# Expert weights in another row order: eight (or four) consecutive rows to a partition

## Chip, cores and metric

One core of a Trainium2 chip runs the whole program in one launch. The metric is the device time in microseconds. TensorE (PE) does the matmuls, VectorE (DVE) and ScalarE (ACT) the elementwise work, GpSimd (POOL) the gathers, and SyncE (SP) issues most loads.

## What is computed

Two transformer blocks on 1024 tokens of 1024 features, all in f32. Around the change it is the first block's modulation and its mixture of experts:

```python
mod = silu(c) @ w_ada + b_ada
shift1, scale1, gate1, shift2, scale2, gate2 = split(mod, 6)
...
h2 = rmsnorm(x, norm2_w) * (1 + scale2) + shift2
...
g = argmax(softmax(h2 @ w_group + b_group))          # 4 groups of 8 experts
e = top_2(softmax(logits of the experts of group g))
xs = h2[tokens sorted by expert]
hid = silu(xs @ w1[e]) * (xs @ w3[e])                # w1, w3: (32, 1024, 512)
ys = (hid @ w2[e]) * gate                            # w2: (32, 512, 1024)
x = x + gate2 * sum_of_the_two(ys)
```

The second block has neighbourhood attention, gated linear attention and a dense MLP. The change does not touch it.

## The kernel before

Everything is tiled to 128 partitions: T = 1024 tokens are NT = 8 tiles, D = 1024 features are NK = 8 tiles, an expert's inner width DE = 512 is four tiles. The program is a sequence of stages. Each ends with a barrier of all engines (meet, line 144); inside a stage the engines run beside each other and wait on semaphores.

**Modulation** (lines 197 to 280). SP loads w_ada in 24 pieces of 1 MB (wa, line 223), and DVE adds each, times silu(c), into acc, 128 partitions by 6144 columns (line 248). TensorE then sums over the partitions: for each of 32 groups of 128 columns a matmul with acc as the stationary operand and a column of ones as the moving one, which gives one column of bank 0 (line 265); after that four matmuls of 512 columns for the two gates (line 270). DVE copies the columns to mod (line 252) and the gates (line 256), and affine_vector makes scale and shift columns of them (lines 278 and 279), with the norm's weights from cols. Column f of such a table holds features 128 f to 128 f + 127, one to a partition.

**Expert pass** (lines 1484 to 1696). The tokens are sorted by expert into blocks of 128 rows, at most 48; how many are in use is known only at run time, and the engines skip the others. For each block:

- SP loads the expert's w1, w3 and w2 (lines 1520, 1521, 1525), 2 MB each, into one of two sets of buffers, and may do so as soon as the block two before has used them. rows (line 1519) reads row 128 k + p of a matrix into partition p, place k: for w1 and w3 a partition gets eight pieces of 2 KB, for w2 four pieces of 4 KB.
- POOL gathers the block's 128 rows of normed x from DRAM (line 1544).
- TensorE turns the rows, eight transposes (experts_turn, line 1553, through the helper transposes, line 346). In a transpose the data is the stationary operand and the identity the moving one. ACT and DVE apply scale and shift while they copy the result to xsT (lines 1624, 1626).
- TensorE multiplies by w1 and w3 in two parts of 256 inner columns each (line 1587, xsT stationary, the weights moving), ACT and DVE make hid, TensorE turns hid (line 1592) and multiplies by w2 (line 1606); the next block's rows are turned between the two halves of hid.

The order on TensorE is the order of the code: up product, half of hid, next block's rows, other half, down product. Names of the trace: e_w is w1, w3 or w2, e_rows the gathered rows, e_xsT the turned ones, e_hid and e_hidT the inner values, mod_acc is acc. An f32 matmul leaves two records of PE and two of its weight load (PEld), a transpose one of each. The first tile named behind the arrow is the moving operand.

The lines that give the two orders before:

```python
rows = lambda w: io[w][ds(e, 1)].squeeze(0).rearrange("(k p) f -> p k f", p=P)
...
t = pe.matmul(experts_up_bank(k, part, j), b.xsT[n][:, f, :], w[:, f, part * HALF:(part + 1) * HALF], start=f == 0, stop=f == NK - 1)
```

Of the kernel before, what the change touches and what calls it, by code (L numbers as in the profile page):

```python
# [11 lines left out]
ALU = mybir.AluOpType  # L12
ACT = mybir.ActivationFunctionType
AX = mybir.AxisListType
ds = bass.ds
# [217 lines left out]
def modulation_vector(k, s, b, mod, gates):  # L233

    v = k.nc.vector
    loaded = (s.wa_0, s.wa_1, s.wa_2, s.wa_3, s.wa_4, s.wa_5)
    v.memset(b.acc[:, :], 0.0).then_inc(*s.acc_zero.up().inc)
    v.wait_ge(*s.acc_zero(1))
    v.wait_ge(*s.ada_bias(1))
    v.wait_ge(*s.c_silu(1))  # L240
    for i in range(NK):
        for j in range(3):
            n = 3 * (i % 2) + j
            v.wait_ge(*loaded[n](i // 2 + 1))
            if i:
                v.wait_ge(*s.ada_step(3 * (i - 1) + j + 1))
            part = b.acc[:, j * 2 * D:(j + 1) * 2 * D]
            v.scalar_tensor_tensor(part, b.wa[n][:, :], b.cT[:, i:i + 1], part, ALU.mult, ALU.add).then_inc(*s.ada_step.up().inc)
    v.wait_ge(*s.columns_made(1))
    for j in (0, 3):  # L250
        part = slice(j * NK, (j + 2) * NK)
        v.tensor_copy(mod[:, part], k.bank[0][:, part]).then_inc(*k.V.up().inc)
    for n in range(2):
        for h in range(2):
            v.wait_ge(*s.gate_made(2 * n + h + 1))
            v.tensor_copy(gates[n][:, h * BANK:(h + 1) * BANK], k.bank[1 + 2 * n + h][:, :]).then_inc(*k.V.up().inc)


def modulation_tensor(k, s, b):

    pe = k.nc.tensor
    pe.wait_ge(*s.ada_step(3 * NK))
    columns = [j for j in range(6 * NK) if j // NK not in (2, 5)]
    for j in columns:
        t = pe.matmul(k.bank[0][:, j:j + 1], b.acc[:, j * P:(j + 1) * P], k.c("ones")[:, 0:1], start=True, stop=True)
    t.then_inc(*s.columns_made.up().inc)
    for n, at in ((0, 2), (1, 5)):
        for h in range(2):
            cols = slice(at * D + h * BANK, at * D + (h + 1) * BANK)
            t = pe.matmul(k.bank[1 + 2 * n + h][:, :], k.c("ones"), b.acc[:, cols], start=True, stop=True)  # L270
            t.then_inc(*s.gate_made.up().inc)


def affine_vector(k, affine, mod, cols):

    v = k.nc.vector
    for n, j in ((0, 0), (1, 3)):
        v.scalar_tensor_tensor(affine[:, 2 * n, :], mod[:, (j + 1) * NK:(j + 2) * NK], 1.0, cols[:, n, :], ALU.add, ALU.mult).then_inc(*k.V.up().inc)
        v.tensor_copy(affine[:, 2 * n + 1, :], mod[:, j * NK:(j + 1) * NK]).then_inc(*k.V.up().inc)
    k.meet()  # L280

# [61 lines left out]
def transposes(k, bank, src, n=4):  # L343

    for h in range(n):
        t = k.nc.tensor.transpose(bank[:, h * P:(h + 1) * P], src[:, h * P:(h + 1) * P], k.c("ident"))  # L346
    return t
# [1158 lines left out]
def experts_sync(k, s, b, experts):  # L1506

    sy, io = k.nc.sync, k.io
    used = used_blocks(sy, experts)
    up, gate, down = (s.up_loaded_0, s.up_loaded_1), (s.gate_loaded_0, s.gate_loaded_1), (s.down_loaded_0, s.down_loaded_1)  # L1510
    for at in range(BLOCKS):
        n = at % 2
        there = used > at
        e = sy.value_load(experts[0:1, at:at + 1], min_val=0, max_val=NE - 1)
        if at >= 2:
            sy.wait_ge(*s.up_made(4 * (at - 1)))
            sy.wait_ge(*up[n](at // 2))
            sy.wait_ge(*gate[n](at // 2))
        rows = lambda w: io[w][ds(e, 1)].squeeze(0).rearrange("(k p) f -> p k f", p=P)
        sy.dma_start(b.w1[n][:, :, :], rows("w1"), cond=there, bounds_check="skip_entire_dma").then_inc(*up[n].up().inc)  # L1520
        sy.dma_start(b.w3[n][:, :, :], rows("w3"), cond=there, bounds_check="skip_entire_dma").then_inc(*gate[n].up().inc)
        if at >= 2:
            sy.wait_ge(*s.down_made(at - 1))
            sy.wait_ge(*down[n](at // 2))
        sy.dma_start(b.w2[n][:, :, :], rows("w2"), cond=there, bounds_check="skip_entire_dma").then_inc(*down[n].up().inc)
    for n in range(2):
        sy.wait_ge(*up[n].now())
        sy.wait_ge(*gate[n].now())
        sy.wait_ge(*down[n].now())
# [20 lines left out]
def experts_turn(k, s, b, n, half):  # L1550

    out = (s.half_0_turned, s.half_1_turned)[half]
    transposes(k, k.bank[half], b.rows[n][:, half * BANK:(half + 1) * BANK]).then_inc(*out.up().inc)


HALF = DE // 2
# [2 lines left out]
def experts_up_bank(k, part, j):  # L1559

    return k.bank[((2, 3), (7, 4))[part][j]][:, 0:HALF]


def experts_tensor(k, s, b, experts):
# [7 lines left out]
    for at in range(BLOCKS):  # L1572
        n = at % 2
        with pe.If(used > at):
            pe.wait_ge(*up[n](at // 2 + 1))
            pe.wait_ge(*s.half_0_out(4 * (at + 1)))
            pe.wait_ge(*s.half_1_out(4 * (at + 1)))
            for part in range(2):
                for j, w in enumerate((b.w1[n], b.w3[n])):
                    if part == 0 and j:  # L1580
                        pe.wait_ge(*gate[n](at // 2 + 1))
                    if at:
                        pe.wait_ge(*(s.hid_ready if j else s.silu_ready)(2 * (at - 1) + part + 1))
                    if at and part == 0 and j == 0:
                        pe.wait_ge(*s.hidT_out(2 * at))
                    for f in range(NK):
                        t = pe.matmul(experts_up_bank(k, part, j), b.xsT[n][:, f, :], w[:, f, part * HALF:(part + 1) * HALF], start=f == 0, stop=f == NK - 1)  # L1587
                    t.then_inc(*s.up_made.up().inc)
            for part in range(2):
                pe.wait_ge(*s.hid_ready(2 * at + part + 1))  # L1590
                for f in (2 * part, 2 * part + 1):
                    t = pe.transpose(k.bank[2 + part][:, f % 2 * P:(f % 2 + 1) * P], b.hid[:, f * P:(f + 1) * P], k.c("ident"))
                t.then_inc(*s.hid_turned.up().inc)
                if part == 0:
                    pe.wait_ge(*got[1 - n]((at + 1) // 2 + 1))
                    experts_turn(k, s, b, 1 - n, 0)
                    experts_turn(k, s, b, 1 - n, 1)
            pe.wait_ge(*down[n](at // 2 + 1))
            for part in range(2):
                pe.wait_ge(*s.hidT_out(2 * at + part + 1))  # L1600
                if at and part == 0:
                    pe.wait_ge(*s.y_out_a(at))
                    pe.wait_ge(*s.y_out_v(at))
                for h in range(2):
                    for f in (2 * part, 2 * part + 1):
                        t = pe.matmul(k.bank[5 + h][:, :], b.hidT[:, f * P:(f + 1) * P], b.w2[n][:, f, h * BANK:(h + 1) * BANK],  # L1606
                                      start=f == 0, stop=f == DE // P - 1)
            t.then_inc(*s.down_made.up().inc)
        with pe.Else():
            pe.drain()  # L1610
            pe.sem_inc(s.up_made.sem, 4)
            pe.sem_inc(s.half_0_turned.sem, 1)
            pe.sem_inc(s.hid_turned.sem, 2)
            pe.sem_inc(s.half_1_turned.sem, 1)
            pe.sem_inc(s.down_made.sem, 1)
# [804 lines left out]
def build(nc, io, out):  # L2420

    with ExitStack() as ctx:
# [9 lines left out]
        xn_rows, y_rows = dram("xn_rows", T, D), dram("y_rows", BLOCKS * P, D)  # L2432
        x_rows = [dram(f"x_rows{n}", T, D) for n in range(3)]
        rpb_rows = dram("rpb_rows", NAH, 2 * KH - 1, W, 2 * W - 1)
        cols = sb("cols", P, 4, NK)
        load_constants(k, consts, cols)

        hT = sb("hT", P, NK, T)
        routed = ctx.enter_context(ExitStack())
        of = lambda name, *shape, dt=F32: routed.enter_context(k.area(name, shape, dt))  # L2440
        mod, affine, gate1, gate2 = of("mod", P, 6 * NK), of("affine", P, 4, NK), of("gate1", P, D), of("gate2", P, D)
        gates, where, tokens, experts = of("gates", P, NT, 2), of("where", P, NT, 2, dt=U32), of("tokens", P, BLOCKS + 1, dt=U32), of("experts", P, BLOCKS + 1, dt=I32)
        with Areas(k) as area:
            x = area("x_first", P, NT, D)
# [15 lines left out]
            store_rows(k, x, x_rows[0])  # L2460
            norm_transpose(k, x, hT, affine[:, 2, :], affine[:, 3, :], xn_dram=xn_rows)
        route(k, hT, gates, where, tokens, experts)
        experts_pass(k, affine[:, 2, :], affine[:, 3, :], tokens, experts, xn_rows, y_rows)
        with Areas(k) as area:
            norm_w, x = area("final_w", P, D), area("x_routed", P, NT, D)
            load_vector(k, norm_w, io["final_norm_w"])
# [23 lines left out]
def arrays_of(inputs):  # L2490
# [7 lines left out]
    io["b_ada"] = a["b_ada"].reshape(1, -1)  # L2498
    io["cT"] = by_feature(a["c"].reshape(-1))
    io["positions"] = a["positions"].reshape(NT, P).T  # L2500
    io["norm_columns"] = np.stack([by_feature(a[n].reshape(-1)) for n in ("norm1_w", "norm2_w", "ln_mix_g_2", "ln_ff_g_2")], 1)
    io["conv"] = a["conv_w"][0].reshape(4, 12, P).transpose(2, 1, 0)
    for n, src in (("a_log", "a_log"), ("dt_bias", "dt_bias"), ("dn_norm_w", "dn_norm_w"), ("b_group", "b_group"),
                   ("b_expert", "b_expert"), ("final_norm_w", "final_norm_w"), ("ln_final_g_2", "ln_final_g_2"),
# [21 lines left out]
```

## Time and profile before

| | us |
|---|---|
| median of 3 runs | 4374.59 |
| lowest, highest | 4372.19, 4376.29 |
| the profiled execution | 4376.07 |
| its span, first to last instruction | 4374.3 |
| modulation, from its last addition on DVE to the last affine column | 85.2 to 105.9 |
| expert pass, first gather's index to the next stage's first load | 1469.9 to 2299.3 |

The profile is of one execution. The span is the time between its first and last instruction; the profiled execution's own time is 1.8 us longer. "Busy" is the time in which an engine executes something; matmuls are pipelined, so the pace of a stream of them is read from the starts of groups in the timeline and not from the mean of one. The granted clock is a share of TensorE's full 2.4 GHz.

### The profile page before, as it was taken

What the parts mean: (1) busy time and instruction counts of PE and PEld (TensorE: products, weight loads), DVE (VectorE), ACT (ScalarE), POOL (GpSimd) and SP (SyncE); (2) the same over time, 40 slices, a digit from 0 to 9 for tenths busy, and PEclk for the clock granted to TensorE, in tenths of its full rate; (3) what the DMA queues carried; (4) which work ended last, traced back from release to release, by engine and by line L of the source; (5) the groups of instructions that cost most, each with busy time, mean ns of one, the idle gap of its engine ahead of it and who ended that gap; (6) DMA issues with size and microseconds to landing.
All of it is one profiled execution on the core that took longest, in us unless ns stands there. A gap on an engine that the chain in (4) does not pass through costs nothing. (4 is left out here: it accounts for less than half of the span.)

```text
span 4374.3 us, 31822 instructions
## 1 busy us (share of the span) xinstructions
PE 3570.6 (82%) x12530; PEld 2143.0 (49%) x12530; DVE 1055.8 (24%) x2157; ACT 697.0 (16%) x1576; POOL 186.1 (4%) x215
## 2 busy tenths in 40 slices
PE   1697789677777699999961877889656899999999
PEld 1344454566634577777741335543443444444444
DVE  6203213444412311111105015600562200000101
ACT  0201101222201122222212015500210100000000
POOL 0002000111000000000011000000000000000000
PEclk9798889777877699999985888899667999999999
DMA  6113411000022598899954210010002111122222
GB/s 282 39 39 49 160 25 34 1 1 1 1 77 79 209 343 334 334 334 334 334 201 158 57 38 1 1 58 5 1 1 77 59 38 39 39 77 86 87 82 77
DMA packets 223732, 457.98 MB, mean 105 GB/s; under 512 B 27120, under 2 KB 80912, under 8 KB 220368
## 3 DMA queue, kind: packets, MB, share of 16 engines
q1 hardware_dynamic: 207409, 396.48, 26.8%
q0 software_dynamic: 9360, 34.08, 2.1%
q10 hardware_dynamic: 6800, 25.17, 1.4%
q8 instruction: 111, 1.82, 0.2%
q14 instruction: 52, 0.43, 0.0%
HBM read 479.43 MB, written 66.82 MB: 125 GB/s over the span
## 5 line engine op out<-in xcount | busy, mean ns | idle before, releaser
L1587 PE MATMUL bank<-e_w,e_xsT 128*128 128x256 f32 x2240 | 492.3, 381 | 6.7 <-DMA e_w<-in_w 6.7
L1587 PEld LDWEIGHTS bank<-e_w,e_xsT 128*128 128x128 f32 x2240 | 427.4, 191 | 80.5 <-issue 16.3
L2316 PE MATMUL bank<-w_ff,uT 128*128 128x512 f32 x1024 | 441.8, 594 | 2.6 <-DVE hT L2368 2.6
L2299 PE MATMUL bank<-hT,w_ff 128*128 128x512 f32 x1024 | 439.7, 592 | 1.3 <-DVEq L149 1.3
L2316 PEld LDWEIGHTS bank<-w_ff,uT 128*128 128x128 f32 x1024 | 195.0, 191 | 249.1 <-issue 244.1
L2299 PEld LDWEIGHTS bank<-hT,w_ff 128*128 128x128 f32 x1024 | 194.5, 190 | 245.9 <-issue 244.4
L464 PE MATMUL bank<-w_out,mixT 128*128 128x512 f32 x512 | 225.0, 603 | 44.0 <-DMA w_out<-in_w_out 44.0
L1606 PE MATMUL bank<-e_w,e_hidT 128*128 128x512 f32 x560 | 246.1, 592 | 0.0
L464 PE MATMUL bank<-w_in,hT 128*128 128x512 f32 x512 | 221.6, 596 | 24.1 <-DMA w_in<-in_w_in 24.1
L346 PE MATMUL bank<-consts,norm_xn 128*128 128x128 f32 x256 | 56.8, 414 | 193.9 <-DVE norm_xn L401 193.9
L464 PEld LDWEIGHTS bank<-w_out,mixT 128*128 128x128 f32 x512 | 99.0, 194 | 169.2 <-issue 169.2
L464 PE MATMUL bank<-w_gla,hT 128*128 128x512 f32 x384 | 166.6, 597 | 11.3 <-DMA w_gla<-in_w_in 11.3
L734 PE MATMUL bank<-hT,w_qkv 128*128 128x512 f32 x384 | 168.6, 598 | 8.6 <-DMA w_qkv<-in_w_in 8.6
L464 PEld LDWEIGHTS bank<-w_in,hT 128*128 128x128 f32 x512 | 97.8, 191 | 147.4 <-issue 147.4
L1606 PEld LDWEIGHTS bank<-e_w,e_hidT 128*128 128x128 f32 x560 | 103.7, 190 | 117.2 <-issue 117.2
L346 PEld LDWEIGHTS bank<-consts,norm_xn 128*128 128x128 f32 x256 | 51.4, 223 | 201.3 <-issue 144.9
L1683 DVE TENSOR_TENSOR e_hid<-e_act,bank 128x256 f32<-128x256 f32 x70 | 29.5, 421 | 455.8 <-PE bank L1587 455.8
L2359 DVE TENSOR_TENSOR uT<-uT,bank 128x512 f32<-128x512 f32 x64 | 41.1, 684 | 400.7 <-ACT uT L2334 400.7
L734 PE MATMUL bank<-hT,w_nqk 128*128 128x512 f32 x256 | 113.0, 605 | 16.9 <-DMA w_nqk<-in_w_in 16.9
L464 PEld LDWEIGHTS bank<-w_gla,hT 128*128 128x128 f32 x384 | 73.5, 192 | 103.8 <-issue 103.8
L734 PEld LDWEIGHTS bank<-hT,w_qkv 128*128 128x128 f32 x384 | 72.9, 192 | 96.4 <-issue 96.4
L2368 DVE TENSOR_TENSOR hT<-hT,bank 128x512 f32<-128x512 f32 x16 | 10.7, 684 | 410.7 <-PE bank L2316 410.6
(448 smaller groups left out, 3967.0 us busy)
## 6 DMA issues: line engine op xcount, KB each, us to landing
e_w<-in_w SPq DMA_DIRECT2D x144, 2048.0 KB
w_ff<-in_w_ff SPq DMA_DIRECT2D x96, 512.0 KB
wa<-in_w_ada SPq DMA_DIRECT2D x24, 1024.0 KB, 12.6
y_rows<-e_y ACTq DMA_DIRECT2D x48, 512.0 KB
y_rows<-r_zero SPq DMA_DIRECT2D x1, 16384.0 KB
w_in<-in_w_in SPq DMA_DIRECT2D x4, 2048.0 KB
w_out<-in_w_out SPq DMA_DIRECT2D x4, 2048.0 KB, 10.5
x_rows<-x_mixed SPq DMA_DIRECT2D x2, 4096.0 KB, 12.8
```

The lines of the kernel that those rows point to most:

```text
L346: t = k.nc.tensor.transpose(bank[:, h * P:(h + 1) * P], src[:, h * P:(h + 1) * P], k.c("ident"))
L464: t = pe.matmul(k.bank[m][:, :], xT[:, f, m * P:(m + 1) * P], wbuf[at % 2][:, f, :], start=f == 0, stop=f == NK - 1)
L734: t = pe.matmul(k.bank[2 * (n % 2) + h][:, :], wbuf[n % 2][:, f, :], xT[:, f, h * BANK:(h + 1) * BANK], start=f == 0, stop=f == NK - 1)
L1587: t = pe.matmul(experts_up_bank(k, part, j), b.xsT[n][:, f, :], w[:, f, part * HALF:(part + 1) * HALF], start=f == 0, stop=f == NK - 1)
L1606: t = pe.matmul(k.bank[5 + h][:, :], b.hidT[:, f * P:(f + 1) * P], b.w2[n][:, f, h * BANK:(h + 1) * BANK], start=f == 0, stop=f == DE // P ...
L1683: v.tensor_tensor(b.hid[:, cols], b.act[:, cols], experts_up_bank(k, part, 1), ALU.mult).then_inc(*s.hid_ready.up().inc)
L2299: t = pe.matmul(k.bank[2 * (j % 2) + h][:, :], w[:, f, :], hT[:, f, h * BANK:(h + 1) * BANK], start=f == 0, stop=f == NK - 1)
L2316: t = pe.matmul(k.bank[2 * n + h][:, :], uT[:, f, m * P:(m + 1) * P], b.ring[j % SLOTS][:, h * BANK:(h + 1) * BANK], start=f == 0, stop=f ...
L2359: v.tensor_tensor(dst, dst, k.bank[2 * (j % 2) + h][:, :], ALU.mult).then_inc(*s.u_ready.up().inc)
L2368: v.tensor_tensor(dst, dst, k.bank[2 * (m % 4) + h][:, :], ALU.add).then_inc(*s.x_added.up().inc)
```

## The change

The weights of an expert are loaded in another row order, and all that depends on it follows:

- rows reads row 8 p + k (w1, w3) or 4 p + k (w2) into partition p, place k. A partition's eight or four rows are one contiguous piece of 16 KB.
- Feature tile f of the block's rows must then hold features f, 8 + f, 16 + f, ...: experts_turn reads every eighth column of the gathered rows.
- Inner tile q must hold inner columns q, 4 + q, ...: the up product reads every fourth column of w1 and w3.
- The affine columns of the expert pass are needed in the new feature order. 16 more column matmuls in the modulation, which read every eighth column of acc, a third copy to mod, and two more operations in affine_vector make them; cols gets a fifth column set. The tables for route and the norm stay.

```diff
-    for j in (0, 3):
+    for j in (0, 3, 6):
         part = slice(j * NK, (j + 2) * NK)
         v.tensor_copy(mod[:, part], k.bank[0][:, part]).then_inc(*k.V.up().inc)
...
     for j in columns:
-        t = pe.matmul(k.bank[0][:, j:j + 1], b.acc[:, j * P:(j + 1) * P], k.c("ones")[:, 0:1], start=True, stop=True)
+        pe.matmul(k.bank[0][:, j:j + 1], b.acc[:, j * P:(j + 1) * P], k.c("ones")[:, 0:1], start=True, stop=True)
+    for j in range(2 * NK):
+        at = (3 + j // NK) * D + j % NK
+        t = pe.matmul(k.bank[0][:, 6 * NK + j:6 * NK + j + 1], b.acc[:, at:at + D - j % NK:NK], k.c("ones")[:, 0:1], start=True, stop=True)
     t.then_inc(*s.columns_made.up().inc)
...
-    for n, j in ((0, 0), (1, 3)):
-        v.scalar_tensor_tensor(affine[:, 2 * n, :], mod[:, (j + 1) * NK:(j + 2) * NK], 1.0, cols[:, n, :], ALU.add, ALU.mult).then_inc(*k.V.up().inc)
+    for n, j, w in ((0, 0, 0), (1, 3, 1), (2, 6, 4)):
+        v.scalar_tensor_tensor(affine[:, 2 * n, :], mod[:, (j + 1) * NK:(j + 2) * NK], 1.0, cols[:, w, :], ALU.add, ALU.mult).then_inc(*k.V.up().inc)
         v.tensor_copy(affine[:, 2 * n + 1, :], mod[:, j * NK:(j + 1) * NK]).then_inc(*k.V.up().inc)
...
-        rows = lambda w: io[w][ds(e, 1)].squeeze(0).rearrange("(k p) f -> p k f", p=P)
+        rows = lambda w: io[w][ds(e, 1)].squeeze(0).rearrange("(p k) f -> p k f", p=P)
...
-    transposes(k, k.bank[half], b.rows[n][:, half * BANK:(half + 1) * BANK]).then_inc(*out.up().inc)
+    for q in range(4):
+        f = half * 4 + q
+        t = k.nc.tensor.transpose(k.bank[half][:, q * P:(q + 1) * P], b.rows[n][:, f:f + D - NK + 1:NK], k.c("ident"))
+    t.then_inc(*out.up().inc)
...
-                        t = pe.matmul(experts_up_bank(k, part, j), b.xsT[n][:, f, :], w[:, f, part * HALF:(part + 1) * HALF], start=f == 0, stop=f == NK - 1)
+                        columns = w[:, f, :].rearrange("p (c q) -> p q c", q=4)[:, 2 * part:2 * part + 2, :]
+                        t = pe.matmul(experts_up_bank(k, part, j), b.xsT[n][:, f, :], columns, start=f == 0, stop=f == NK - 1)
...
-        experts_pass(k, affine[:, 2, :], affine[:, 3, :], tokens, experts, xn_rows, y_rows)
+        experts_pass(k, affine[:, 4, :], affine[:, 5, :], tokens, experts, xn_rows, y_rows)
```

On TensorE at the start of the program, where the columns (mod_acc stationary) and the gates (mod_acc moving) are made, the order before is

```order
L265 MATMUL bank<-consts,mod_acc 128x1 x32
L270 MATMUL bank<-mod_acc,consts 128x512 x4
L346 MATMUL bank<-consts,norm_xn_1 128x128 x64
L464 MATMUL bank<-w_in_1,hT 128x512 x256
L346 MATMUL bank<-consts,r_qk_1 128x128 x16
```

and with the change

```order
L265 MATMUL bank<-consts,mod_acc 128x1 x32
L268 MATMUL bank<-consts,mod_acc 128x1 x16
L273 MATMUL bank<-mod_acc,consts 128x512 x4
L349 MATMUL bank<-consts,norm_xn_1 128x128 x64
L467 MATMUL bank<-w_in_1,hT 128x512 x256
L349 MATMUL bank<-consts,r_qk_1 128x128 x16
```

The 16 new matmuls stand between the old columns and the gates; what follows is in the old order, at line numbers three higher and more.

On TensorE in the expert pass, from the branch that begins block 0, the order before is

```order
L346 MATMUL bank<-consts,e_rows_1 128x128 x8
L1574 COMPARE_AND_BRANCH
L1587 MATMUL bank<-e_w_1,e_xsT_1 128x256 x32
L1592 MATMUL bank<-consts,e_hid 128x128 x2
L346 MATMUL bank<-consts,e_rows_1 128x128 x8
L1592 MATMUL bank<-consts,e_hid 128x128 x2
L1606 MATMUL bank<-e_w_1,e_hidT 128x512 x8
L1574 UNCONDITIONAL_BRANCH
L1609 UNCONDITIONAL_BRANCH
L1574 COMPARE_AND_BRANCH
```

and with the change

```order
L1558 MATMUL bank<-consts,e_rows_1 128x128 x8
L1580 COMPARE_AND_BRANCH
L1594 MATMUL bank<-e_w_1,e_xsT_1 128x256 x32
L1599 MATMUL bank<-consts,e_hid 128x128 x2
L1558 MATMUL bank<-consts,e_rows_1 128x128 x8
L1599 MATMUL bank<-consts,e_hid 128x128 x2
L1613 MATMUL bank<-e_w_1,e_hidT 128x512 x8
L1580 UNCONDITIONAL_BRANCH
L1616 UNCONDITIONAL_BRANCH
L1580 COMPARE_AND_BRANCH
```

Number, kinds and order are the same; the turned rows now come from the loop in experts_turn and not from the helper transposes.

## Rows read from the trace of the kernel before

**Rows 1.** The page, parts 1 and 2: busy time, and the clock in 40 slices.
```profile
span 4374.3 us, 31822 instructions
...
PE 3570.6 (82%) x12530; PEld 2143.0 (49%) x12530; DVE 1055.8 (24%) x2157; ACT 697.0 (16%) x1576; POOL 186.1 (4%) x215
...
PEclk9798889777877699999985888899667999999999
```

**Rows 2.** Windows, two stretches: stretch, length, busy by engine, granted clock, DMA share, GB/s.
```profile
1522.00:1544.00 22.00, 22.00 (x93) 16.47 (x93) 2.90 (x7) 4.81 (x10) 1.15 (x2) 1.00 1.04 400
1600.00:1800.00 200.00, 200.00 (x840) 149.99 (x839) 26.08 (x63) 43.65 (x91) 10.29 (x18) 1.00 0.90 335
```

**Rows 3.** Timeline of PE, a block: start, us, engine, line, operation, tiles, shapes, count.
```profile
1508.86 13.98 PE L1587 MATMUL bank<-e_w,e_xsT 128*128 128x256 f32 x64
1522.67 0.38 PE L1592 MATMUL bank<-consts,e_hid 128*128 128x128 f32 x2
1522.89 1.04 PE L346 MATMUL bank<-consts,e_rows 128*128 128x128 f32 x8
...
1523.98 7.03 PE L1606 MATMUL bank<-e_w,e_hidT 128*128 128x512 f32 x16
1530.85 13.98 PE L1587 MATMUL bank<-e_w,e_xsT 128*128 128x256 f32 x64
```

**Rows 4.** The page, part 5: the costliest group, its count and mean.
```profile
L1587 PE MATMUL bank<-e_w,e_xsT 128*128 128x256 f32 x2240 | 492.3, 381 | 6.7 <-DMA e_w<-in_w 6.7
```

**Rows 5.** Waits of PE from 1470 to 2257 us: total, times, longest.
```profile
PE bank L1587 <- DMA e_w<-in_w: 6.7, 2, 6.0
PE bank L346 <- DMA e_rows<-xn_rows,e_idx: 5.6, 1, 5.6
```

**Rows 6.** Timeline of all engines, start of the expert pass.
```profile
1470.32 1.15 POOL L1544 DMA_INDIRECT e_rows<-xn_rows,e_idx  x1 [0.29 <-POOL e_idx L1542]
...
1471.54 0.42 SPq L1520 DMA_DIRECT2D e_w<-in_w  x1
...
1475.10 1.97 PE L346 MATMUL bank<-consts,e_rows 128*128 128x128 f32 x8 [5.64 <-DMA e_rows<-xn_rows,e_idx]
...
1477.11 1.37 DVE L1624 TENSOR_SCALAR e_xsT<-bank,affine 128x128 f32<-128x128 f32 x4 [7.40 <-PE bank L346]
...
1483.07 6.49 PE L1587 MATMUL bank<-e_w,e_xsT 128*128 128x256 f32 x16 [5.99 <-DMA e_w<-in_w]
...
1490.22 10.63 PE L1587 MATMUL bank<-e_w,e_xsT 128*128 128x256 f32 x48 [0.66 <-DMA e_w<-in_w]
```

**Rows 7.** Timeline of all engines, end of the modulation.
```profile
85.35 13.73 PEld L265 LDWEIGHTS bank<-consts,mod_acc 128*128 128x128 f32 x64 [85.35 <-issue]
...
99.03 5.59 PE L270 MATMUL bank<-mod_acc,consts 128*128 128x512 f32 x8
...
105.49 0.17 DVE L278 SCALAR_TENSOR_TENSOR affine<-mod,cols 128x8 f32<-128x8 f32 x1
...
105.73 0.16 DVE L279 COPY affine<-mod 128x8 f32<-128x8 f32 x1
```

**Rows 8.** Packets and bytes, 30 to 60 us, 1490 to 1500 us, 1471 to 1484 us.
```profile
DMA packets 1738, 12.66 MB, mean 422 GB/s; under 512 B 193, under 2 KB 193, under 8 KB 193
...
DMA packets 1627, 3.94 MB, mean 394 GB/s; under 512 B 31, under 2 KB 31, under 8 KB 1627
...
DMA packets 1730, 4.20 MB, mean 323 GB/s; under 512 B 50, under 2 KB 50, under 8 KB 1730
...
q1 hardware_dynamic: 1327, 2.68, 57.9%
q0 software_dynamic: 403, 1.51, 32.6%
```

**Rows 9.** Timeline of POOL, a gather in mid-pass, and its tile's time to landing.
```profile
1502.46 0.96 POOL L1544 DMA_INDIRECT e_rows<-xn_rows,e_idx  x1 [0.27 <-POOL e_idx L1542]
...
DMA to landing us min/median/max: 4.1/7.8/8.9
```

More of the change, by code:

```diff
@@ L2434, in build @@
         rpb_rows = dram("rpb_rows", NAH, 2 * KH - 1, W, 2 * W - 1)
-        cols = sb("cols", P, 4, NK)
+        cols = sb("cols", P, 5, NK)
         load_constants(k, consts, cols)
@@ L2440, in build @@
         of = lambda name, *shape, dt=F32: routed.enter_context(k.area(name, shape, dt))
-        mod, affine, gate1, gate2 = of("mod", P, 6 * NK), of("affine", P, 4, NK), of("gate1", P, D), of("gate2", P, D)
+        mod, affine, gate1, gate2 = of("mod", P, 8 * NK), of("affine", P, 6, NK), of("gate1", P, D), of("gate2", P, D)
         gates, where, tokens, experts = of("gates", P, NT, 2), of("where", P, NT, 2, dt=U32), of("tokens", P, BLOCKS + 1, dt=U32), of("experts", P, BLOCKS + 1, dt=I32)
@@ L2500, in arrays_of @@
     io["positions"] = a["positions"].reshape(NT, P).T
-    io["norm_columns"] = np.stack([by_feature(a[n].reshape(-1)) for n in ("norm1_w", "norm2_w", "ln_mix_g_2", "ln_ff_g_2")], 1)
+    io["norm_columns"] = np.stack([by_feature(a[n].reshape(-1)) for n in ("norm1_w", "norm2_w", "ln_mix_g_2", "ln_ff_g_2")] + [vec("norm2_w").reshape(P, NK)], 1)
     io["conv"] = a["conv_w"][0].reshape(4, 12, P).transpose(2, 1, 0)
```

## Prediction

> **What bounds the kernel now.** I read the page first: one core, a span of 4374.3 us, TensorE busy for 3570.6 us of it, and a clock that is granted in full over the middle of the span [rows 1]. The change touches two places, so I then asked for each by itself: the expert pass (1470 to 2299 us) and the modulation at the start (85 to 106 us).
>
> In the expert pass the windows show TensorE busy 200.00 us of 200.00, at a granted clock of 1.00 (2.4 GHz), while the DMA engines are at 0.90 and move 335 GB/s [rows 2]. The timeline of PE gives the pulse: one block's up product starts at 1508.86 us and the next at 1530.85, so a block takes 21.99 us, and the rows between join without a gap [rows 3]. There are 35 blocks in use: 2240 records of L1587 [rows 4] at 64 a block (32 matmuls, two records each for f32). The table of waits says what TensorE waited for in the whole pass: 6.7 us, in two waits, for expert weights, and 5.6 us for the first gathered rows [rows 5]. So **the whole of what faster weight loads can give in this pass is 6.7 us**, 0.15% of the span; all other loads of weights already land under matmuls. What can cost is any change in what TensorE itself does, 35 times over.
>
> In the modulation nothing overlaps: DVE waits for the column matmuls, then for the gate matmuls, then makes the affine columns, and a barrier holds everybody. What TensorE needs longer there is longer for the kernel [rows 7].
>
> **The change, part by part.**
>
> *Loads in one piece of 16 KB a partition (w1, w3, w2).* In mid-pass: nothing. The load rate is not what a block waits for. After the start the engines catch up at 400 GB/s with pieces of 2 and 4 KB [rows 2], more than the 335 GB/s that a block's pulse asks for. At the start of the pass there is something to win. w1's first load is issued at 1471.54 us and TensorE starts on it at 1483.07; w3 costs 0.66 us more at 1490.22 [rows 6]. The nearest rows for the rate are these: pieces of 2 and 4 KB at 394 GB/s (1490 to 1500 us), pieces of 8 KB in the w_ada loads at 422 GB/s (30 to 60 us), and 4.20 MB moved between 1471 and 1484 us, of which 1.51 MB for gathers [rows 8]. The lower bound of the gain is 0. The upper is 4.6 + 0.7 = 5.3 us: the turned rows are ready at 1477.11 + 1.37 = 1478.48 us [rows 6], so w1 cannot be used before that, 4.6 us earlier than now. I take −1.5 us: 2.68 MB of queue 1 at 422 in place of 394 GB/s saves 0.45 us, the second wait of 0.66 goes, and 0.4 because larger pieces take a larger share from the gathers beside them. The other side of this last point is that the gathers land later. In mid-pass they have the time: one is issued at 1502.46 us, lands after a median of 7.8 us, and is first needed at 1522.89 [rows 3, 9]. The first gather landed at 1475.10 and could slip some 3 us before w1 is no longer last.
>
> *Turned rows (L346 in the pass becomes a loop in experts_turn).* As many transposes, with a stationary operand whose 128 elements lie 32 bytes apart in place of side by side. Now 12 transposes take 1523.98 − 1522.67 = 1.31 us, 0.109 us each [rows 3]. Lower bound 0, upper bound: the weight load takes twice as long and shows in full, 8 × 0.109 × 35 = 31 us. I take 0, for the reason under the next edit.
>
> *Inner columns (L1587).* As many matmuls, but the moving operand reads every fourth element, 16 bytes apart. One record of 256 columns now takes 13.98 / 64 = 0.218 us, one of 512 columns (L1606) 6.87 / 16 = 0.429 us [rows 3]: 0.82 ns for a column of f32, two cycles of the 2.4 GHz clock. No matmul in this trace has a step in its operands, so both ends stay open. Lower bound 0; upper bound, each element takes twice as long: 2240 × 0.218 = 489 us. I take 0. TensorE takes an element only every second cycle, and it does so wherever the clock is granted; the slack for another address is there. That is an inference from the pace, not a row, and it is the weakest step. The Trainium skill speaks against it: "Advanced Engine Details and Errata", section "SBUF Cachelines", says that lines have 16 bytes and that at least two hits on a line are needed to hide the access latency. Here each f32 element would be the only hit on its line; by that rule the upper bound of 489 us, not zero, is the one to take, which makes the sum about +495 us, and no row here shows it.
>
> *Modulation.* It gets 16 more column matmuls of one column, 32 records. The 64 records there now take 13.73 us on the weight-load side, 0.2145 us each [rows 7]; 32 more are +6.9 us on the path. Bounds: at the pace of the fast transposes, 0.109, only +3.5; with the step of 32 bytes in the weight load costing double, +13.7. I take 6.9, since these rows are the same instruction in the same place. On DVE a third copy to mod hides while DVE waits for the gate matmuls; the two more affine operations add 0.16 us (four of them start between 105.49 and 105.73). Sum **+7.0 us**. The cols load is 4 KB larger: nothing.
>
> *Experts' affine columns, hid, w2 and y.* The same shapes on the same engines, with other numbers inside: 0.
>
> *The end of the pass* (the unused blocks) skips the loads of weights, so they cannot shorten it.
>
> **Sum:** +7.0 − 1.5 = +5.5 us. The profiled execution took 4376.07 us (span 4374.3) and would become 4381.6; the median of the three runs, 4374.59, lies 1.5 us below that execution, so the forecast for the median is 4380. I call 0.2% (8.75 us) what a measurement of this kernel can tell from no change. So the forecast is: no change that can be told, on the slow side. Own range of this case: 4374 to 4386.
>
> **Rivals.**
>
> 1. *Slower: the stepped moving operand.* Place: L1587 (L1594 in the changed kernel). Price: 0.218 us for each of 2240 records if reading at a step of 16 bytes halves the pace, 489 us, and with the weight loads of the turned rows (31) and of the modulation (6.9) it is 527: 4380 + 527 = 4907. It decides from about 2% of loss per matmul on (2% of 489 is 9.8 us). For it: no row shows a stepped operand at the present pace. Against it: two cycles per element. Chance 0.12. (The rule of the Trainium skill quoted above, "SBUF Cachelines", would make this case the forecast.)
>
> 2. *Slower, the weight load alone.* Only the stationary operand at 32 bytes is slow, while the moving one is not: 31 + 6.9 = 38 us more, 4418. The transposes have no long matmul to hide a weight load under, which the up product has. Chance 0.08.
>
> 3. *Slower, in between.* Either a partial loss on the moving operand (10% is 49 us: 4429), or the loads of 16 KB run slower than those of 2 KB because 128 pieces that lie 16 KB apart suit the memory less. That decides below 335 GB/s; at 300 a block would need 24.6 us, 35 × 2.6 = 90 us: 4470. Nothing in the trace speaks for the latter, pieces of 8 KB being the fastest [rows 8]. Chance 0.06.
>
> 4. *Faster.* The start of the pass gives its full 5.3 us and the added column matmuls cost 3.5 + 0.2: −1.6 us, 4373. Still no change that can be told. To be faster by over 8.75 us more must go than TensorE ever waits for in the pass, so this holds only what I do not see, chance 0.05 in all. That the larger pieces do nothing for the loads at all is inside the forecast: 4381.5.
>
> **How the numbers follow.** The forecast has 0.69, the rivals 0.12, 0.08, 0.06 and 0.05. The forecast's case lies within 0.2% but for some 0.02 at its slow end. Faster 0.04, same 0.68, slower 0.28. The range takes the forecast's case with its bounds and rival 2, and leaves out rivals 1 and 3 (0.18): 4370 to 4420. It is 4380 because that is the likeliest case, not a mean.
>
> **What would show it.** Right: a block's pulse still 21.99 us and 64 records of the up product in 13.98; 12 transposes in 1.31 us; 96 weight-load records of about 0.2145 us in the modulation, with its gate matmuls starting near 105.9 us in place of 99.03; TensorE's first up product 1 to 2 us sooner after w1's issue, and the second wait gone; the packets of queue 1 fewer by tens of thousands. Wrong: a pulse over 22 us without a wait (rival 1 or 2, told apart by which rows are longer), or one with waits for DMA inside the pass (rival 3); a modulation shorter than 12 us for its 96 records would make my largest term half as big.

## The result, and the profile after

| | before | changed |
|---|---|---|
| median us | 4375.44 (4 runs, 4372.19 to 4377.42) | 4906.86 (4 runs, 4904.24 to 4915.14) |
| ratio to before | | 1.1219, 95% interval 1.1199 to 1.1238 |
| profiled execution, its span | 4376.07, 4374.3 | 4904.24, 4902.4 |

The change makes the kernel 531 us slower. The page of the changed kernel, against [rows 1]: the span, busy times, the clock, and the packets of the queue that carries the weights.

```profile
span 4902.4 us, 31889 instructions
...
PE 4104.9 (84%) x12562; PEld 2189.4 (45%) x12562; DVE 1056.1 (22%) x2160; ACT 697.0 (14%) x1576; POOL 185.9 (4%) x215
...
PEclk9897798878869999999999859888976799999999
...
q1 hardware_dynamic: 131249, 396.48, 22.9%
```

TensorE is busy for 534 us more, with 32 records more. The clock is granted in full over more slices than before. The weights come in 131249 packets in place of 207409 on the page of before, so the loads did change as meant:

```profile
q1 hardware_dynamic: 207409, 396.48, 26.8%
```

The costliest group of the page is the up product, as in [rows 4]:

```profile
L1594 PE MATMUL bank<-e_w,e_xsT 128*128 128x256 f32 x2240 | 1021.4, 632 | 3.7 <-DMA e_w<-in_w 3.7
```

As many records, 2240, but a mean of 632 ns where it was 381. Ahead of them the engine waits 3.7 us in all. The timeline of PE shows the pulse of a block, to be laid beside [rows 3]:

```profile
1481.68 29.64 PE L1594 MATMUL bank<-e_w,e_xsT 128*128 128x256 f32 x64 [3.68 <-DMA e_w<-in_w]
...
1519.35 29.17 PE L1594 MATMUL bank<-e_w,e_xsT 128*128 128x256 f32 x64
1548.35 0.40 PE L1599 MATMUL bank<-consts,e_hid 128*128 128x128 f32 x2
1548.58 1.06 PE L1558 MATMUL bank<-consts,e_rows 128*128 128x128 f32 x8
1549.48 0.38 PE L1599 MATMUL bank<-consts,e_hid 128*128 128x128 f32 x2
1549.70 7.03 PE L1613 MATMUL bank<-e_w,e_hidT 128*128 128x512 f32 x16
1556.57 29.17 PE L1594 MATMUL bank<-e_w,e_xsT 128*128 128x256 f32 x64
```

From one up product to the next it is 1556.57 − 1519.35 = **37.22 us**, where it was 21.99. The up product itself goes from 13.81 us (1508.86 to 1522.67) to 29.00, so a record from 0.216 us to 0.453, 1.77 ns a column (paces are taken from start to start). The twelve transposes from 1548.35 to 1549.70 take 1.35 us, where they took 1.31. The windows and the waits of the pass (columns as in [rows 2, 5]) show that in mid-pass neither the clock nor a load is missing:

```profile
1481.00:1484.00 3.00, 2.32 (x5) 1.75 (x6) 0.00 (x0) 0.00 (x0) 0.00 (x0) 0.50 1.03 412
...
1600.00:1800.00 200.00, 200.00 (x492) 94.98 (x491) 14.92 (x36) 24.42 (x51) 5.72 (x10) 1.00 0.49 196
```

```profile
PE bank L1594 <- DMA e_w<-in_w: 3.7, 1, 3.7
```

In the middle TensorE is busy all the time at a clock of 1.00, while the DMA engines have fallen to half their time. The first load of the pass and the end of the modulation, as in [rows 6, 7]:

```profile
1472.51 0.36 SPq L1523 DMA_DIRECT2D e_w<-in_w  x1
```

```profile
85.18 13.73 PEld L265 LDWEIGHTS bank<-consts,mod_acc 128*128 128x128 f32 x64 [85.18 <-issue]
...
98.79 7.71 PEld L268 LDWEIGHTS bank<-consts,mod_acc 128*128 128x128 f32 x32
...
106.44 5.07 PE L273 MATMUL bank<-mod_acc,consts 128*128 128x512 f32 x8
...
113.03 0.16 DVE L282 COPY affine<-mod 128x8 f32<-128x8 f32 x1
```

The first load is issued at 1472.51 us and used at 1481.68, after 9.17 us in place of 11.53, and TensorE has no second wait of its own. The rows of 1490 to 1500 us, with the loads at full flow, as in [rows 8]:

```profile
DMA packets 309, 4.32 MB, mean 432 GB/s; under 512 B 43, under 2 KB 43, under 8 KB 46
```

That is 432 GB/s with pieces of 16 KB, against 394 with 2 and 4 KB and 422 with 8 KB.

**Where the 528.1 us of the spans lie.** The last affine column starts at 113.03 in place of 105.73: +7.3. From there to the first load of w1, in stages that the change doesn't touch, 1359.5 us against 1365.8: −6.3, the scatter of single executions. From that load to the first up product: −2.4. From the first up product to the end of the last down product 1303.1 us against 773.7 us: +529.4. After it 2117.6 against 2117.5: +0.1. Of the 529.4, 34 blocks give 34 × 15.22 = 517.5 and the first block 11.9, because before that block was slow too: it ran in part at a granted clock of 0.50.

### The profile page after: what moved, and what is told of

Same layout as the page of the kernel before. It is cut to its first block and busy times, and to the rows that moved or that the text cites. A ratio compares the mean times of both kernels' runs of the same rounds, so it can differ in the third digit from the quotient of the medians.

```text
span 4902.4 us, 31889 instructions
## 1 busy us (share of the span) xinstructions
PE 4104.9 (84%) x12562; PEld 2189.4 (45%) x12562; DVE 1056.1 (22%) x2160; ACT 697.0 (14%) x1576; POOL 185.9 (4%) x215
## 3 DMA queue, kind: packets, MB, share of 16 engines
q1 hardware_dynamic: 131249, 396.48, 22.9%
## 5 line engine op out<-in xcount | busy, mean ns | idle before, releaser
L1594 PE MATMUL bank<-e_w,e_xsT 128*128 128x256 f32 x2240 | 1021.4, 632 | 3.7 <-DMA e_w<-in_w 3.7
L1594 PEld LDWEIGHTS bank<-e_w,e_xsT 128*128 128x128 f32 x2240 | 467.4, 209 | 550.2 <-issue 544.3
L1653 ACT ACTIVATE e_act<-bank 128x256 f32<-128x256 f32 x70 | 26.8, 383 | 654.9 <-PE bank L1594 654.9
```

The lines of the kernel that those rows point to most:

```text
L1653: a.activation(b.act[:, part * HALF:(part + 1) * HALF], experts_up_bank(k, part, 0), ACT.Silu).then_inc(*s.silu_ready.up().inc)
```

## The experiments

The theory after the result (A): a moving operand with a step of 16 bytes is read at half the pace or less, and nothing else of the change matters. Rivals: the loads in large pieces disturb TensorE's reading (B); the pattern of two dimensions does it, not the step (C). The pulse of a block and the pace of its 64 records are the measure, since they don't depend on the stages ahead. All profile rows below are of PE's timeline, but for one of SP in experiment 1. Experiments 2 and 9 edit the kernel before, with its loads; the others edit the changed one and keep w1 and w3 in pieces of 16 KB. Experiments 2, 5, 6, 7 and 8 leave out what would make the columns match again, so their output is another one; the amount of work is the same. Where a kernel ran once, its rows carry the argument and not its time: the kernel before took 4368 to 4402 us in the 30 runs made beside experiments 1 to 6, 8 and 10.

**1. The step undone, the large pieces kept.**

```diff
-columns = w[:, f, :].rearrange("p (c q) -> p q c", q=4)[:, 2 * part:2 * part + 2, :]
+columns = w[:, f, part * HALF:(part + 1) * HALF]
...
+tiles = io["w2"][ds(e, 1)].squeeze(0).rearrange("(k p) f -> p k f", p=P)
...
-sy.dma_start(b.w2[n][:, :, :], rows("w2"), ...)
+sy.dma_start(b.w2[n][:, :, :], tiles, ...)
```

> The changed kernel with the inner columns undone: the up product reads 256 neighbouring columns of w1 and w3 as before, and w2 goes back to four pieces of 4 KB a partition to match. Loads of w1 and w3 stay in pieces of 16 KB, turned rows and modulation stay as changed. Theory A (all of the loss is the 16-byte step in the moving operand): one record of the up product back to 0.216 us, the pulse of a block at 22.03 us (the turned rows keep their 0.04), time 4375.4 + 7.4 for the modulation + 1.4 for the turned rows - 3 for the start of the pass = about 4381. Theory B (the loads of 16 KB pieces into the partitions that TensorE reads slow it down): the records stay near 0.45 us and the time near 4900.

Measured: 4376.7 us (10 runs) against 4372.11 (13 runs), ratio 1.0006, interval 0.9996 to 1.0015.

```profile
1472.86 0.36 SPq L1524 DMA_DIRECT2D e_w<-in_w  x1
...
1482.12 6.11 PE L1595 MATMUL bank<-e_w,e_xsT 128*128 128x256 f32 x16 [3.77 <-DMA e_w<-in_w]
1489.91 10.63 PE L1595 MATMUL bank<-e_w,e_xsT 128*128 128x256 f32 x48 [1.67 <-DMA e_w<-in_w]
...
1508.57 13.98 PE L1595 MATMUL bank<-e_w,e_xsT 128*128 128x256 f32 x64
1522.38 0.38 PE L1600 MATMUL bank<-consts,e_hid 128*128 128x128 f32 x2
...
1530.57 13.98 PE L1595 MATMUL bank<-e_w,e_xsT 128*128 128x256 f32 x64
```

The pulse is 22.00 us and the up product 13.81 us again. Theory B falls: with w1 and w3 in pieces of 16 KB TensorE keeps its old pace. One more thing shows here. w1 is used 9.3 us after its issue and not 11.5, but then TensorE waits 1.67 us for w3, so the start of the pass wins less than the first wait says: the second up product begins 1508.57 − 1472.86 = 35.71 us after the first load, where it was 1508.86 − 1471.54 = 37.32, 1.6 us less.

**2. The step alone, in the kernel before.**

```diff
-... b.xsT[n][:, f, :], w[:, f, part * HALF:(part + 1) * HALF], ...
+columns = w[:, f, :].rearrange("p (c q) -> p q c", q=4)[:, 2 * part:2 * part + 2, :]
+... b.xsT[n][:, f, :], columns, ...
```

> The kernel before with one edit: the up product reads every fourth column of w1 and w3. Loads, turned rows and modulation as before. It leaves the match with w2's rows out, so that the output is another one. Theory A: 0.453 us a record, 29.0 us for the up product of a block, a pulse of 37.2 us, time 4375 + 35 x 15.19 = about 4907. Theory B (the loads do it, not the step): 0.216 us a record and 4375.

Measured: one run, 4901.41 us.

```profile
1516.31 29.17 PE L1588 MATMUL bank<-e_w,e_xsT 128*128 128x256 f32 x64
1545.30 0.40 PE L1593 MATMUL bank<-consts,e_hid 128*128 128x128 f32 x2
...
1553.50 29.17 PE L1588 MATMUL bank<-e_w,e_xsT 128*128 128x256 f32 x64
```

28.99 us for the up product and a pulse of 37.19: this one edit makes the whole loss, with the loads of before. With experiment 1 this settles where it comes from.

**3. A step of 8 bytes.**

```diff
+pairs = io["w2"][ds(e, 1)].squeeze(0).rearrange("(t p k) f -> p t k f", t=2, k=2)
...
-columns = w[:, f, :].rearrange("p (c q) -> p q c", q=4)[:, 2 * part:2 * part + 2, :]
+columns = w[:, f, part * HALF:(part + 1) * HALF].rearrange("p (c q) -> p q c", q=2)
```

> The changed kernel with a step of two columns (8 bytes) in place of four (16 bytes); w2's rows are loaded to match, in two pieces of 8 KB. Theory A1 (the time goes by 16-byte lines, 1.77 ns for each new line, as measured at one element a line): two elements a line are 0.885 ns an element against 0.843 now, 0.227 us a record, a pulse of about 22.8 us, time about 4406. Theory A2 (any step at all, elements that are not neighbours, takes the slow way): 0.453 us a record, time about 4907. A3 (cost in proportion to the step): about 0.30 us a record, 4570.

Measured: one run, 4400.52 us.

```profile
1508.09 14.67 PE L1595 MATMUL bank<-e_w,e_xsT 128*128 128x256 f32 x64
1522.60 0.38 PE L1600 MATMUL bank<-consts,e_hid 128*128 128x128 f32 x2
...
1530.80 14.67 PE L1595 MATMUL bank<-e_w,e_xsT 128*128 128x256 f32 x64
```

14.51 us for 64 records, 0.2267 us each: A1's number. A step as such is not what costs (A2), nor does the cost grow in proportion (A3).

**4. Two dimensions without a step.**

```diff
+tiles = io["w2"][ds(e, 1)].squeeze(0).rearrange("(k p) f -> p k f", p=P)
...
-columns = w[:, f, :].rearrange("p (c q) -> p q c", q=4)[:, 2 * part:2 * part + 2, :]
+columns = w[:, f, :].rearrange("p (q h c) -> p h q c", q=2, h=2)[:, part, :, :]
...
-... b.w2[n][:, f, h * BANK:(h + 1) * BANK], ...
+... b.w2[n][:, f % 2 * 2 + f // 2, h * BANK:(h + 1) * BANK], ...
```

> The changed kernel with the moving operand in two dimensions as there (2 by 128), but without a step: two runs of 128 neighbouring columns, 256 apart; w2 in its old order, its tiles taken to match. Theory A: 0.216 us a record, time about 4381 as for the kernel without a step. Theory C (the pattern of two dimensions costs, not the step): 0.453 us a record, time about 4907.

Measured: one run, 4392.31 us.

```profile
1522.13 13.98 PE L1595 MATMUL bank<-e_w,e_xsT 128*128 128x256 f32 x64
1535.94 0.38 PE L1600 MATMUL bank<-consts,e_hid 128*128 128x128 f32 x2
```

The up product takes 13.81 us, so theory C falls. The time is 11 us above what was expected, and none of it is in the pass: its first up product starts at 1495.60 us and not at about 1482, behind stages that are the same in all these kernels. A single run's time can be that far off (4368 to 4402 us for the kernel before); the pulse of before is 21.99 us at each of its steady blocks.

**5. A step of 12 bytes.**

```diff
-columns = w[:, f, :].rearrange("p (c q) -> p q c", q=4)[:, 2 * part:2 * part + 2, :]
+whole = w[:, f, :]
+columns = bass.AP(whole.tensor, whole.offset + part, [list(whole.ap[0]), [P, 2], [3, P]])
```

> The changed kernel with a step of three columns (12 bytes) in the up product's moving operand: two runs of 128 elements, the second 128 columns on. It multiplies by columns that overlap and don't match w2, so that the output is another one. Theory A1 (1.77 ns for each new 16-byte line): four elements touch three lines, 0.75 x 1.77 = 1.33 ns an element, 0.34 us a record, 64 records in 21.8 us, a pulse of about 30.0 us, time about 4660. Theory A4 (full pace while at least one of two neighbours shares a line, else the slow way): between, a line with one element costs 1.77 and a line with two 1.69, the same 0.34. Theory A5 (every step above 8 bytes goes the slow way, element by element): 0.453 us a record, time about 4905.

Measured: one run, 4658.68 us.

```profile
1518.02 21.91 PE L1595 MATMUL bank<-e_w,e_xsT 128*128 128x256 f32 x64
1539.76 0.39 PE L1600 MATMUL bank<-consts,e_hid 128*128 128x128 f32 x2
...
1547.97 21.92 PE L1595 MATMUL bank<-e_w,e_xsT 128*128 128x256 f32 x64
```

21.74 us, 0.3397 us a record, where 0.75 lines an element at 1.77 ns gave 0.340 (A1). A5 falls. A4 is not "the same 0.34" when its own prices are multiplied out: two lines with one element and one with two are 2 × 1.77 + 1.69 = 5.23 ns for four elements, 0.335 us a record, and for a step of 8 bytes it has the full pace, 0.216, where experiment 3 measured 0.227. So A1 fits better, by 0.005 and 0.011 us a record.

**6. A step of 32 bytes.**

```diff
-columns = w[:, f, :].rearrange("p (c q) -> p q c", q=4)[:, 2 * part:2 * part + 2, :]
+columns = w[:, f, :].rearrange("p (c q) -> p q c", q=8)[:, 4 * part:4 * part + 4, :]
```

> The changed kernel with a step of eight columns (32 bytes) in the moving operand, four runs of 64; hid's columns no longer match w2's rows, so that the output is another one. Theory A1 (time by the line): each element is a new line as with 16 bytes, 0.453 us a record, a pulse of 37.2 us, time about 4905. Theory A3 (cost grows with the distance): clearly above, 0.6 us or more a record, time above 5200.

Measured: one run, 4922.13 us.

```profile
1518.49 29.69 PE L1594 MATMUL bank<-e_w,e_xsT 128*128 128x256 f32 x64
1547.99 0.40 PE L1599 MATMUL bank<-consts,e_hid 128*128 128x128 f32 x2
...
1556.21 29.68 PE L1594 MATMUL bank<-e_w,e_xsT 128*128 128x256 f32 x64
```

29.50 us, 0.461 us a record: twice the distance costs 1.7% more, not twice as much, and A1, which had 0.453, is off by that much. A3 falls for good. Since this operand is four runs of elements where the change has two, another kernel was made to tell the number of runs from the distance.

**7. The same with four runs.**

```diff
-columns = w[:, f, :].rearrange("p (c q) -> p q c", q=4)[:, 2 * part:2 * part + 2, :]
+columns = w[:, f, :].rearrange("p (h c q) -> p h q c", h=2, q=4)[:, :, 2 * part:2 * part + 2, :]
```

> The changed kernel with the same step of 16 bytes in the up product, but as four runs of 64 elements and not two of 128; hid's columns then don't match w2's rows, so that the output is another one. The step of 32 bytes in e6_step_8 also had four runs, and took 0.461 us a record and not 0.453. Theory H (each further run costs a few ns): 0.461 us, time about 4920. Theory I (the distance costs, not the run): 0.453 us, about 4905.

Measured: one run, 4916.16 us (the pass began 12 us later than in the changed kernel).

```profile
1531.96 29.18 PE L1594 MATMUL bank<-e_w,e_xsT 128*128 128x256 f32 x64
1560.96 0.40 PE L1599 MATMUL bank<-consts,e_hid 128*128 128x128 f32 x2
```

29.00 us: the number of runs costs nothing (H falls), so the 1.7% belong to the distance (I).

**8. The step on the stationary operand.**

```diff
-columns = w[:, f, :].rearrange("p (c q) -> p q c", q=4)[:, 2 * part:2 * part + 2, :]
+columns = w[:, f, part * HALF:(part + 1) * HALF]
+turned = b.xsT[n][:, :, :].rearrange("p k c -> p (k c)")[:, f:f + D - NK + 1:NK]
-... b.xsT[n][:, f, :], columns, ...
+... turned, columns, ...
```

> The kernel of e1_no_step with a step of 32 bytes in the up product's stationary operand in place of one in the moving one: it reads every eighth element of the turned rows, 128 of them. It mixes features, so that the output is another one. Theory D (the weight load reads stepped elements at nearly its own pace, as the turned rows' transposes at 0.112 us show, and hides under the matmul of 0.216 us): 0.216 us a record, a pulse of 22.0 us, time as e1_no_step, about 4377. Theory E (1.77 ns a line holds for the weight load as well): 128 elements take 0.227 us, longer than the matmul's 0.216, 64 records in 14.5 us, a pulse of 22.7 us, time about 4401.

Measured: one run, 4433.93 us.

```profile
1514.52 15.45 PE L1596 MATMUL bank<-e_w,e_xsT 128*128 128x256 f32 x64
1529.80 0.38 PE L1601 MATMUL bank<-consts,e_hid 128*128 128x128 f32 x2
...
1538.00 15.45 PE L1596 MATMUL bank<-e_w,e_xsT 128*128 128x256 f32 x64
```

15.28 us, 0.2388 us a record. Theory D falls and E holds in kind, though it had 0.227 us a record and 4401 us: 128 stepped elements of a weight load take 0.239 us (1.87 ns each, not 1.77), which no longer hides under the matmul's 0.216 us. It costs 1.47 us a block against 15.19, since the load has 128 stepped elements and not 256, and only what is longer than the matmul shows. The 32 added column matmuls of the modulation, whose stationary operand has the same step, give the same 0.238 us a record. D was drawn from the turned rows, and these are transposes.

**9. The step on the identity of the transposes.**

```diff
+k.nc.vector.tensor_copy(k.ident4[:, 0:4 * P - 3:4], k.c("ident")).then_inc(*k.V.up().inc)
...
-transposes(k, k.bank[half], b.rows[n][:, half * BANK:(half + 1) * BANK]).then_inc(*out.up().inc)
+    t = k.nc.tensor.transpose(k.bank[half][:, q * P:(q + 1) * P], b.rows[n][:, f * P:(f + 1) * P], k.ident4[:, 0:4 * P - 3:4])
```

> The kernel before, contiguous everywhere, but the turned rows' transposes take their moving operand, the identity, from a table with every element 16 bytes from the next (made by DVE at the start of the pass, with one more barrier). Theory F (a stepped read takes about 0.885 ns whoever makes it, and an f32 matmul reads each element of an operand twice, a transpose once): 128 x 0.885 = 0.113 us a transpose against 0.109, the eight of a block in about 0.91 us, a pulse of 22.03 us, time about 4378. Theory G (a stepped element costs the moving side 1.77 ns in any instruction): 0.227 us a transpose, eight in 1.8 us, a pulse of 22.9 us, time about 4408.

Measured: one run, 4408.4 us (the kernel before, once beside it, 4387.5).

```profile
1508.87 13.98 PE L1595 MATMUL bank<-e_w,e_xsT 128*128 128x256 f32 x64
...
1522.90 2.02 PE L1560 MATMUL bank<-e_ident,e_rows 128*128 128x128 f32 x8
1524.74 0.40 PE L1600 MATMUL bank<-consts,e_hid 128*128 128x128 f32 x2
...
1531.85 13.98 PE L1595 MATMUL bank<-e_w,e_xsT 128*128 128x256 f32 x64
```

The eight transposes take 1.84 us, 0.230 each, and the pulse is 22.98 us: theory G. That the time meets its 4408 us says little with one run. A moving operand pays some 1.8 ns for each stepped element in a transpose as in a matmul. The idea that an f32 matmul pays double because it reads everything twice and a transpose once (F) does not hold for the moving side. A stationary operand with 32 bytes pays 0.1125 us at most in a transpose (0.90 us for the eight in the changed kernel) and 0.239 in an f32 matmul; why these two differ stays open.

**10. Large pieces with every step on a transpose's stationary side.** w2 comes in pieces of 8 KB. The 16 added columns of the modulation are gone; the affine columns in the new order come through DRAM instead.

```diff
+pairs = io["w2"][ds(e, 1)].squeeze(0).rearrange("(t p k) f -> p t k f", t=2, k=2)
...
+columns = w[:, f, part * HALF:(part + 1) * HALF]
...
-pe.transpose(..., b.hid[:, f * P:(f + 1) * P], k.c("ident"))
+pe.transpose(..., b.hid[:, part * HALF + f % 2:(part + 1) * HALF - 1 + f % 2:2], k.c("ident"))
...
-for j in range(2 * NK):
-    at = (3 + j // NK) * D + j % NK
-    t = pe.matmul(k.bank[0][:, 6 * NK + j:6 * NK + j + 1], b.acc[:, at:at + D - j % NK:NK], k.c("ones")[:, 0:1], start=True, stop=True)
...
+k.nc.sync.dma_start(dram.rearrange("a (k p) -> p a k", p=P), affine[:, 2:4, :], ...)
+k.nc.sync.dma_start(affine[:, 4:6, :], dram.rearrange("a (p k) -> p a k", k=NK))
```

> A version that keeps large pieces and has no step in a moving operand: w1 and w3 in pieces of 16 KB, the up product contiguous, w2 in two pieces of 8 KB, hid turned with a step of two in the stationary operand, and the affine columns for the new order made without TensorE, by a small store and load through DRAM on SP under the first norm. Theory A: against before 0 for the modulation, -1.7 to -3 us for the start of the pass, +1.4 for the turned rows (35 x 0.04), about +0.5 for hid: 4371 to 4376 where before is 4374, no difference that can be told. Rival: TensorE never waited for loads but 6.7 us, yet the larger pieces also shorten other waits; then it is faster by more than 9 us.

Measured: 4374.75 us (12 runs) against 4380.08 (17 runs), ratio 0.9986, interval 0.9971 to 1.0002.

```profile
1501.41 13.98 PE L1602 MATMUL bank<-e_w,e_xsT 128*128 128x256 f32 x64
1515.23 0.39 PE L1607 MATMUL bank<-consts,e_hid 128*128 128x128 f32 x2
...
1523.46 13.98 PE L1602 MATMUL bank<-e_w,e_xsT 128*128 128x256 f32 x64
```

No difference that can be told from before. The interval, −12.7 to +0.9 us, does not shut out the rival's 9 us by itself; the trace does. The pulse is 22.05 us, 0.06 over before, 1.9 us in 34 blocks. Against that stand 1.3 us at the start of the pass: the second up product begins 36.04 us after the first load of w1 (issued at 1465.37 us) in place of 37.32. From that load to the end of the last down product it is 785.8 us where it was 785.2. So this order of the weights won nothing, in a pass where TensorE waits 6.7 us for them.

## Why the prediction was wrong

**The bound of the pass** was read rightly: TensorE sets the pulse, and faster loads can give at most the 6.7 us it waited. In experiments 1 and 10, with the loads changed and no step in a moving operand, the time is that of before.

**The step that failed** is the one under "Inner columns": "I take 0. TensorE takes an element only every second cycle [...] the slack for another address is there." It was called the weakest step, and it bore the forecast all the same. Measured: 0.453 us for a record in place of 0.216, 2240 times: 532 us, less 3 in the first block. The slack is not there. The pace of contiguous elements could not show it: at 0.84 ns each, four to a line of 16 bytes, they ask for a new line every 3.4 ns, and the step asks for one with every element. The runs fit a price of 1.77 ns for each new line, wherever that is more than the 0.84 ns of its elements: steps of 8, 12, 16 and 32 bytes give 0.227, 0.340, 0.453 and 0.461 us a record. The Trainium skill's rule ("Advanced Engine Details and Errata", section "SBUF Cachelines"), that at least two hits on a 16-byte line are needed, agrees in kind with these rows: with two elements a line the loss is 5%, with one it is 110%. The prediction quoted this rule as speaking against the change and gave it 0.12. (Its "0.82 ns for a column" is a slip: 0.429 us for 512 columns is 0.84. Its 0.218 us a record includes the modelled end of the group; from start to start it is 0.216. Neither moves the forecast.) With no row on either side, a stated rule that names this very pattern should have weighed more than an inference from the pace of contiguous reads.

**Rival 1** named the mechanism, the place and the sign of the profile (a longer pulse without a wait). Its 4907 us meet the 4906.86 measured partly by luck. It had +489 for the moving operand, where 35 × 15.19 = 532 less some 3 for the first block was measured; +31 for the turned rows, where at most 35 × 0.04 = 1.4 was; and +13.9 for the modulation, where +7.3 was. The untouched stages added −6.3 in the profiled execution. The first was too small, since the loss is to 2.1 times and not double, and the other two were too large.

**Turned rows**, taken at 0: right within 1.4 us. The twelve transposes take 0.04 us more a block; the pulse of the changed kernel is over that of experiment 2, whose rows are turned as before, by only 0.02 to 0.03 us (37.22 and 37.21 against 37.19).

**Modulation**, taken at +7.0: +7.3. The 32 added records take 7.6 us, 0.238 us each and not 0.2145; the gate matmuls behind them took 5.07 us and not 5.59, because TensorE came to its full pace after the third of their eight records and not after the fourth (0.85 us a record until then, 0.43 after it).

**Start of the pass**, taken at −1.5: −1.6 in experiment 1. w1 is used 2.3 us sooner after its issue and its 16 records take 0.4 less (6.11 us against 6.49), but 1.0 goes back into the wait for w3 (1.67 us against 0.66), which the prediction had as gone.

**The forecast's own case**, 4380, was +5.5 on before. Experiment 1 is that case but for w2's pieces: +4.6 on before in the medians, +2.6 by the ratio, with an interval of −1.7 to +6.6 us that holds both 0 and +5.5. So the times can't prove the small terms; the rows above bear them out. The step in the moving operand, taken at 0, put the result outside the range.

## What to carry to other kernels

Look at the innermost step of a moving operand before the loads: f32 elements 16 bytes apart more than double a matmul's time, 8 bytes apart cost 5%. If a layout needs a step somewhere, it belongs on the stationary side of a transpose, where 32 bytes cost 0.03 us for eight of them here (0.90 against 0.87). And a load order is worth at most the time that somebody waits for the loads; here that was 6.7 us of 4374.

## What the runs showed that I had not expected

- The stepped read does not follow TensorE's clock. The start of the first block ran at a granted clock of 0.50 (1.2 GHz) in both kernels. The first two lines are of the kernel before, ten records apart; the next two of the changed kernel, four records apart; the last is a window of before (the window of the changed kernel stands above):

```profile
1483.65 5.90 PE L1587 MATMUL bank<-e_w,e_xsT 128*128 128x256 f32 x15
1487.92 1.63 PE L1587 MATMUL bank<-e_w,e_xsT 128*128 128x256 f32 x5
...
1482.30 6.07 PE L1594 MATMUL bank<-e_w,e_xsT 128*128 128x256 f32 x13
1484.11 4.26 PE L1594 MATMUL bank<-e_w,e_xsT 128*128 128x256 f32 x9
...
1484.00:1488.60 4.60, 4.60 (x12) 3.62 (x11) 0.00 (x0) 0.00 (x0) 0.00 (x0) 0.50 1.03 384
```

  A contiguous record takes 4.27 / 10 = 0.427 us there, twice its 0.216 at 1.00; a stepped one 1.81 / 4 = 0.453, as at 1.00. So the step costs 110% at the full clock and 6% at half of it. The stationary side shows the same: the stepped weight loads of the modulation, where the gate matmuls behind them still ran at 0.85 us a record, take 0.238 us, and those of experiment 8 at 1.00 take 0.239. (The windows view gives 1.00 for the modulation too, but the pace of the gate matmuls, 0.85 us a record and then 0.43, says that it was half at first.)
- Up to a step of 16 bytes the price goes by the 16-byte line touched, closely: 0.227 and 0.340 us were worked out for steps of 8 and 12 bytes from the price for 16, and 0.2267 and 0.3397 were measured. That a line has 16 bytes shows in the rows too: below a step of 16 bytes the price grows with the step, and from 16 to 32 it adds 1.7%.
- In the same operand position a transpose and an f32 matmul pay differently on the stationary side (at most 0.1125 against 0.239 us for 128 elements 32 bytes apart), but alike on the moving side (1.80 against 1.77 ns an element).
- SP issued its third load of weights in 0.38 us in the changed kernel (1473.44 us), where the same issue took 6.18 us before (1472.67 us). TensorE did not wait for that load (w2) in either.
